# Two equal tiles handled in one operation in the recurrent branch, and the norms' reciprocal root as a square root and a reciprocal

## The reference

```python
h = rmsnorm(x, norm_mix)                 # x * rsqrt(mean(x^2) + 1e-6) * g
u_pool | u_rnn | u_gate | g_pool | g_rnn = h @ w_in
y_pool = pool_mixer(u_pool) @ w_pool_out
v  = conv4(u_rnn)                        # causal, per channel, 4 taps
r, i = sigmoid(v @ w_a + b_a), sigmoid(v @ w_x + b_x)     # 8 heads of 128 x 128
a  = exp(-8 r softplus(-lam));  b = sqrt(1 - a^2) * i * v
hr_t = a_t * hr_(t-1) + b_t              # along the sequence
y_rnn = (hr * gelu(u_gate)) @ w_rnn_out
x  = x + (sigmoid(g_pool) * y_pool + sigmoid(g_rnn) * y_rnn) @ w_o
h  = rmsnorm(x, norm_ffn);  x = x + (silu(h @ w_gate) * (h @ w_up)) @ w_down    # 2816 wide
out = rmsnorm(x, norm_final)
```

## Time and profile before

| | us |
|---|---|
| median of 3 runs (lowest, highest) | 1024.84 (1024.12, 1025.46) |
| profiled execution, device time | 1024.35 |
| its span, slowest core (core 3, role b) | 1022.8 |
| PE / DVE / ACT / POOL busy on core 3 | 924.4 / 591.4 / 556.7 / 336.8 |

### The profile page before, as it was taken

One profiled execution on the slowest core, in us unless ns is written; L12 is line 12 of the kernel. 1 busy time (PEld: TensorE's weight loads), 2 busy tenths in 40 slices (PEclk: granted clock), 3 DMA queues, 4 the chain that ended last, 5 costly groups with the idle time before them and its releaser, 6 DMA issues.

```text
span 1022.8 us, 13708 instructions; the slowest of 8 cores (1016.8 to 1022.8 us)
## 1 busy us (share of the span) xinstructions
PE 924.4 (90%) x4484; PEld 446.6 (44%) x4484; DVE 591.4 (58%) x798; ACT 556.7 (54%) x804; POOL 336.8 (33%) x347
## 2 busy tenths in 40 slices
PE   2378688698978999999999999999999999999995
PEld 1134233233433444444444444444555555555553
DVE  2179998999999867844253544533644452222235
ACT  2579997989889942548264938611722351111112
POOL 2438593778655641151001122112251211000000
PEclk8579789899989999999999999999999999999998
DMA  8921452003644276768403257255939175910003
GB/s 176 242 69 33 160 93 42 12 1 55 116 82 87 38 192 118 160 98 150 82 8 56 39 80 141 44 101 123 253 69 212 30 129 108 211 41 2 1 1 135
DMA packets 42765, 96.88 MB, mean 95 GB/s; under 512 B 3776, under 2 KB 19264, under 8 KB 42560
## 3 DMA queue, kind: packets, MB, share of 16 engines
q0 software_dynamic: 23904, 63.45, 36.1%
q1 hardware_dynamic: 18784, 32.48, 10.6%
HBM read 151.75 MB, written 7.60 MB: 156 GB/s over the span
## 4 chain that ended last, share of the span: by engine, by line
PE 78%; ACT 9%; issue 5%; POOL 3%; DVE 2%; DMA 2%; ACTq 0%; DVEq 0%; SPq 0%; POOLq 0%
PE bank L705 74%; PE bank L770 2%; PE bank L667 2%; DMA wu<-w_in 2%; ACT th L780 1%; DVE v L757 1%; ACT q L798 1%; POOL sq L638 1%; ACT th L788 1%; ACT v L745 1%; ACT L798 1%; ACT L780 1%; DMA xt<-xT 1%; POOL vb L765 1%; ACT wi L780 0%
## 5 line engine op out<-in xcount | busy, mean ns | idle before, releaser
L705 PE MATMUL bank<-h,wf 128*128 128x508 bf16 (+2 forms) x1408 | 280.7, 358 | 0.0
L705 PEld LDWEIGHTS bank<-h,wf 128*128 128x128 bf16 x1408 | 136.5, 97 | 139.9 <-issue 0.8
L757 DVE SCALAR_TENSOR_TENSOR v<-bank,keep_cst,v 128x496 f32<-128x496 f32 (+3 forms) x200 | 128.8, 683 | 32.4 <-POOL v L754 13.4
L705 PE MATMUL bank<-h,wu 128*128 128x500 bf16 (+4 forms) x576 | 130.1, 381 | 16.3 <-DMA wu<-w_in 11.0
L1084 DVE TENSOR_TENSOR ff<-tf,bank 128x508 bf16<-128x508 f32 (+2 forms) x88 | 55.7, 634 | 147.9 <-PE bank L705 123.5
L705 PE MATMUL bank<-ff,wz 128*128 128x508 bf16 (+2 forms) x704 | 139.5, 359 | 0.0
L1079 ACT ACTIVATE tf<-bank 128x508 f32<-128x508 f32 (+2 forms) x88 | 48.8, 557 | 137.8 <-PE bank L705 134.4
L652 ACT ACTIVATE sq<-x 128x508 f32<-128x508 f32 (+2 forms) x56 | 32.9, 590 | 125.3 <-DVE x L1096 97.4
L705 PEld LDWEIGHTS bank<-ff,wz 128*128 128x128 bf16 x704 | 68.9, 98 | 68.6 <-issue 0.5
L705 PEld LDWEIGHTS bank<-h,wu 128*128 128x128 bf16 x576 | 58.7, 103 | 83.9 <-issue 32.9
L765 POOL CAST vb<-v 128x496 bf16<-128x496 f32 (+3 forms) x68 | 61.1, 905 | 61.4 <-DVE v L757 53.3
(11 more groups left out here) (103 smaller groups left out, 1311.7 us busy)
## 6 DMA issues: line engine op xcount, KB each, us to landing
wf<-wfi POOLq DMA_DIRECT2D x44, 512.0 KB, 9.5
wz<-wfo POOLq DMA_DIRECT2D x16, 704.0 KB, 10.1
xt<-xT SPq DMA_DIRECT2D x16, 500.0 KB, 8.6
wu<-w_in POOLq DMA_DIRECT2D x16, 256.0 KB, 13.7
xt<-xT SPq DMA_DIRECT2D x8, 512.0 KB, 21.1
wa<-w_in POOLq DMA_DIRECT2D x16, 256.0 KB, 5.9
wg<-w_in POOLq DMA_DIRECT2D x16, 256.0 KB, 5.4
wb<-w_in POOLq DMA_DIRECT2D x16, 256.0 KB, 5.5
```

Source lines behind the costliest of these rows:

```text
L705: last = e.matmul(p.tensor[:, 0:n], lhsT=wap(kc), rhs=rhs(kc), start=(kc == 0), stop=(kc == K - 1))
L757: g.op("dve", c_dve(w), k, lambda e, p=p, o=o, w=w, s=s: e.scalar_tensor_tensor(out=v.tensor[:, o:o + w], in0=p.tensor[:, HALO - s:HALO - ...
```

## The change

1. `rnn_pair` (new): where a group has exactly two tiles of one width, and neither the extra tap on POOL (`tap`) nor the PSUM variant (`ps`) is on, both tiles' u groups are written to two neighbouring banks, and each operation on ACT, DVE and POOL up to the tanh is issued once for both. The matmuls stay one per tile.
2. The norm's root: ACT's Sqrt in place in PSUM, then DVE's reciprocal in place, for Ln and Exp on ACT. All norms are changed, 18 in role a and 17 in role b.
3. The gate weights `rg` are loaded in four pieces of two heads, the first in the head, the others when their heads are due. PSUM is one tensor of eight banks; single banks are taken beside occupied ones so that pairs stay free.
4. New tables of numbers. Role b: prefix groups of one, two and two tiles (256; 496 + 496; 496 + 496), own tiles 508 + 508 and 420 + 420, the extra tap for two heads of the last chunk (before: all eight), the PSUM variant off. Role a: tiles 256, 352, 396 and 344, 500, 392 (before 256, 412, 396 and 344, 500, 332); never two tiles in a group, so nothing is joined there.

```diff
+    def find_bank(self, b, t):
+        free = [self.bank_live[i] is None and self.banks[i][0] <= t for i in range(8)]
+        if b.space == "ps2":
+            c = [(max(self.banks[i][0], self.banks[i + 1][0]), i) for i in range(0, 8, 2) if free[i] and free[i + 1]]
+        else:
+            c = [(self.bank_live[i ^ 1] is None, self.banks[i][0], i) for i in range(8) if free[i]]
+        return min(c)[-1] if c else None
...
-                head.append(self.load("pool", rg, lambda: rg.tensor[:], dr["rg"], 128 * 2048 * 4, K, "rg"))
+                head.append(self.load_rg(0, K))
+    def load_rg(self, i, key):
+        b = self.rg[i]
+        return self.load("pool", b, lambda: b.tensor[:], self.dr["rg"][:, 2 * i:2 * i + 2], 128 * 512 * 4, key, "rg")
...
-        ln = self.buf("ln", [w])
-        g.op("act", c_act(w, 1), key, lambda e: e.activation(out=ln.tensor[:], in_=pss.tensor[:, 0:w], func=AF.Ln,
-                                                             bias=self.eps.tensor[:, 0:1]), rd=[pss, self.eps], wr=[ln],
-             table=LN, tag=tag + "ln")
-        g.op("act", c_act(w), key, lambda e: e.activation(out=pss.tensor[:, 0:w], in_=ln.tensor[:], func=AF.Exp, scale=-0.5),
-             rd=[ln], wr=[pss], table=EXPL, tag=tag + "rs")
+        g.op("act", c_act(w, 1), key, lambda e: e.activation(out=pss.tensor[:, 0:w], in_=pss.tensor[:, 0:w], func=AF.Sqrt,
+                                                             bias=self.eps.tensor[:, 0:1]), rd=[pss, self.eps], wr=[pss],
+             table=SQRT, tag=tag + "rs")
+        g.op("dve", c_dve(w), key, lambda e: e.reciprocal(out=pss.tensor[:, 0:w], in_=pss.tensor[:, 0:w]), rd=[pss], wr=[pss], tag=tag + "rc")
...
+        both = len(tiles) == 2 and tiles[0][1] == tiles[1][1] and not (ps or on[2] or on[5])
+        if both:
+            self.rnn_pair(j, tiles, wu, key, toff, v, th, wi, kk_vb)
...
+    def rnn_pair(self, j, tiles, wu, key, toff, v, th, wi, cast):
+        two = lambda b: b.tensor[:].rearrange("p (t w) -> p t w", t=2)
+        p = self.banks("ps_u")
...
+        for s in (1, 2, 3):
+            g.op("dve", c_dve(2 * w), k, lambda e, s=s: e.scalar_tensor_tensor(
+                out=two(v), in0=p.tensor[:, :, HALO - s:HALO - s + w],
+                scalar=cst.tensor[:, C_CW + 8 * (3 - s) + j:C_CW + 8 * (3 - s) + j + 1], in1=two(v),
+                op0=ALU.mult, op1=ALU.add), rd=pk + [cst] + vk, wr=vk, tag="cv")
...
+        for q, hcol, dst in ((0, 0, th), (1, 8, wi)):
+            pg = self.banks("ps_g")
+            for i in range(2):
+                g.op("pe", c_mm(w) + 0.05, k + 1 + 0.3 * q, lambda e, pg=pg, q=q, i=i: e.matmul(
+                    pg.tensor[:, i, 0:w], lhsT=self.rg[j // 2].tensor[:, j % 2, q, :], rhs=vb.tensor[:, i * w:i * w + w], start=True, stop=True),
+                    rd=[vb, self.rg[j // 2]], wr=[(pg, i)], tag="gt")
+            g.op("act", c_act(2 * w, 1), k + 1 + 0.3 * q, lambda e, pg=pg, dst=dst, hcol=hcol: e.activation(
+                out=two(dst), in_=pg.tensor[:, :, 0:w], func=AF.Tanh, scale=0.5,
+                bias=self.hb.tensor[:, hcol + j:hcol + j + 1]), rd=[(pg, 0), (pg, 1), self.hb], wr=[(dst, 0), (dst, 1)], table=TANH, tag="th")
...
-        prefix=[256, 496, 496, 496, 496], groups=[2, 2, 1], own=[[508, 508], [460, 380]], wp=261.84, window2=107.54,
+        prefix=[256, 496, 496, 496, 496], groups=[1, 2, 2], own=[[508, 508], [420, 420]], wp=294.7, window2=309.7,
```

More of the change, by code:

```diff
@@ L164, in can_alloc @@
                 continue
-            if b.space == "ps":
-                if not any(self.bank_live[i] is None and self.banks[i][0] <= t for i in range(8)):
+            if b.space != "sb":
+                if self.find_bank(b, t) is None:
                     return False
@@ L169, in can_alloc @@
                 n += b.nbytes
-        if room and any(b.space == "ps" and b.left is not None for b in o.bufs):
+        if room and any(b.space != "sb" and b.left is not None for b in o.bufs):
             room = 0
@@ L179, in do_alloc @@
             b.left = b.uses
-            if b.space == "ps":
-                c = [(self.banks[i][0], i) for i in range(8) if self.bank_live[i] is None and self.banks[i][0] <= t]
-                _, i = min(c)
-                self.bank_live[i] = b
-                b.off = i
-                extra += self.banks[i][1]
+            if b.space != "sb":
+                i = b.off = self.find_bank(b, t)
+                for x in range(i, i + (2 if b.space == "ps2" else 1)):
+                    self.bank_live[x] = b
+                    extra += self.banks[x][1]
             else:
@@ L203, in finish_refs @@
                         us[u.eng] = u
-                    self.banks[b.off] = (b.dead + self.prm["bank_lag"], list(us.values()))
+                    for x in range(b.off, b.off + (2 if b.space == "ps2" else 1)):
+                        self.bank_live[x] = None
+                        self.banks[x] = (b.dead + self.prm["bank_lag"], list(us.values()))
                 elif b.name.startswith("keep"):
@@ L542, in start @@
         self.xt0 = self.tile8("xt", W0 + HALO)
-        self.rg = rg = self.buf("keep_rg", [2, 8, 128], BF16)
+        self.rg = [self.buf("keep_rg", [2, 2, 128], BF16) for _ in range(4)]
         head = self.load_tile(self.xt0, 0, W0 + HALO, -99, "xt")
@@ L700, in norm1_tile, with mm_group @@
         return h
[L702 removed]
+    def mm_group(self, p, n, wb, rhs, rd, key, tag, K=8, wap=None, half=None):
         def f(e):
             for kc in range(K):
[L705 removed]
+                last = e.matmul(p.tensor[:, 0:n] if half is None else p.tensor[:, half, 0:n], lhsT=wap(kc), rhs=rhs(kc), start=(kc == 0), stop=(kc == K - 1))
             return last
[L707 removed]
+        return self.g.op("pe", K * c_mm(n), key, f, rd=rd + [wb], wr=[p if half is None else (p, half)], tag=tag)
     def proj(self, wb, h, w, key, tag, halo=False, sl=None):
@@ L737, in rnn_group @@
         off = 0
-        for i, (h, w, part) in enumerate(tiles):
+        both = len(tiles) == 2 and tiles[0][1] == tiles[1][1] and not (ps or on[2] or on[5])
+        if both:
+            self.rnn_pair(j, tiles, wu, key, toff, v, th, wi, kk_vb)
+        for i, (h, w, part) in enumerate([] if both else tiles):
             k = key + toff * i
@@ L941, in build @@
         P = prm.get("pre")
+        base, step = (P["rnn"][0] if P else prm["keys"][0]["rnn"])[:2]
+        for i in range(1, 4):
+            self.load_rg(i, base + step * 2 * i - prm["lead"])
         for i, w in enumerate(prm["prefix"]):
@@ L1197, in build_program @@
     with ExitStack() as es:
-        ps = [es.enter_context(nc.psum_tensor("bank%d" % i, [128, 512], F32)) for i in range(8)]
+        ps = es.enter_context(nc.psum_tensor("bank", [128, 8, 512], F32))
         sems = {e: es.enter_context(nc.semaphore("s_" + e)) for e in ENGINES}
@@ L1213, in build_program @@
                     seen.add(id(b))
-                    if b.space == "ps":
-                        b.tensor = ps[b.off]
+                    if b.space != "sb":
+                        b.tensor = ps[:, b.off, :] if b.space == "ps" else ps[:, b.off:b.off + 2, :]
                     else:
```

95 lines of the change are left out of this document (55 added, 40 removed).

## The result

| | us |
|---|---|
| before, median of 4 runs beside it (lowest, highest) | 1024.52 (1024.12, 1025.46) |
| after, median of 4 runs (lowest, highest) | 1067.22 (1064.49, 1068.62) |
| after / before | 1.0408, 95% interval 1.0388 to 1.0429 |
| profiled execution of after | 1066.01, span 1064.2 (core 5, role b) |

What follows compares the result with a forecast made beforehand. DVE, with ACT close behind, was taken to pace role b before about 350 us. -12.5 - 6 + 21.7 - 2 + 4.1 + 4.2 = 9.5 us on 1024.35 gave 1034; range 1015 to 1046, own case 1028 to 1044.

Steps and rivals of the forecast that it cites:

- the gain of 20.5 us: Role b's three gains together: 12.5 us from joined taps, 6 from ACT, 2 from the start.
- At one pass: Rival: reciprocals cost one or two passes; role b's sum becomes -16 us, role a ends last, about 1018; chance 0.24.
- what I called covered: Role b: first two of the stage's seven reciprocals hidden by other waits; later norms hidden behind 68 matmuls or more.
- Joined taps, -12.5: Role b's DVE-paced stage: 72 fewer DVE instructions at 0.17 us each give 12.5 us less.
- the pair as a delay: Rival: late fifth weight and waiting for two norms cost 8 us at role b's start; 1044, up to 1050; chance 0.13.
- ACT, -6: Role b's stage: ACT stops being a second bound; 6 us less, between 0 and 8, bounded by DVE's waits for ACT.
- Start, -2: Role b's start: later first wide tap against DVE work done earlier; 2 us less, from 8 less to 8 more.
- eight passes: Assumed DVE reciprocal cost, 4.3 us at 500 columns; five in role b's stage add 21.7 us; own case, chance 0.50.
- the sign: The whole kernel gets slower, given chance 0.67; faster 0.25, within 0.2% 0.08.
- the hole ahead of the first `wf` group: Role b after the stage: PE stands 4.1 us since only 32 `wo` matmuls cover the second norm's chain.
- The tail's sum: Role b behind the last matmul: wider last tile, reciprocal for Exp and less cover; together 4.2 us more.
- the first `wr` at 367 to 372 us: Expected sign in role b: when PE starts its first `wr` matmul at the stage's end; 367.7 before the change.

Runs made afterwards that it cites:

- e1: Kernel after, same instruction order, each reciprocal replaced by a one-pass multiplication by 1.0 (values differ): 1033.1 us, 1.0084 of before.
- e9: Kernel after with Ln and Exp for the norms, joined pairs kept, role a's old tile widths, order searched anew: 1.0125 of before.
- e13: Kernel after with nothing joined, Ln and Exp for the norms, role a's old tile widths, order searched anew: 1.0026 of before.
- e2: Kernel after, same order, but DVE takes its role's branch ahead of the first reciprocal: 1.0401 of before.
- e3: Kernel after, same order, but rg loaded in one transfer in the head, not four pieces: 1.0340 of before.
- e12: Kernel after, same order, with one pass for each reciprocal and rg in one transfer: 1.0072 of before.
- e11: Kernel after with its reciprocals, role a's old tile widths, order searched anew with the reciprocal's measured price: 1.0190 of before.
- e6: Kernel after, same order, with Ln and Exp on ACT again in place of root and reciprocal: 1.0173 of before.

## Why the prediction was wrong

**The step that failed is the gain of 20.5 us that I set against the reciprocals: 12.5 for the joined taps, 6 for ACT, 2 for the start.** At one pass I had role b 16 us faster; e1 measures that case as 8.6 us slower, an error of 25 of the 33 us that the forecast missed. The other 8 lie in what I called covered among the reciprocals.

- *Joined taps, -12.5.* The count and the rows were right (72 fewer instructions, 1.24 us each), and in place the pairs are worth 9 to 10 us. The price was taken as path, though, since DVE was busy for 95% of the stretch. A pair also has to wait for both of its halves, and the order for pairs in the groups [1, 2, 2] holds that wait: DVE's 10.5 us came back as idle time (e9 against e13), 6.8 of them at the first taps, and the kernel lost 10. I had this rival ("the pair as a delay") with 0.13 and put it at the start alone.
- *ACT, -6.* ACT's work fell as forecast (84 table loads on core 5 for my 86, 38 us less busy in the stretch), and no run shows a gain from it: DVE's wait for ACT's first product, which bounded the gain, rose from 4.6 to 11.3 us on core 5 of after, e9 alike:

```profile
DVE v L874 <- ACT v L869: 11.3, 5, 6.8
```

- *Start, -2.* The first wide tap came at 98.0, not at some 81 (64.5, 8 more, and two reciprocals of 4.3). DVE had done 30 us more by then (46.5 us busy up to 98.0, before 16.6 up to 64.5), 8.3 of them in three reciprocals; so 11.8 us are lost there, 3.5 of them as idle time. The branch is not in it (e2); rg is, with up to 7 us on the slowest core, as long as the reciprocals fill DVE (e3, e12).

**The reciprocals.** Per instruction I was too high (4.3 for 3.27 us at 500), in total too low: from eight passes to one I reckoned 25.4 us, and from six measured passes to one it was 33 to 34 (e1). The error is in what I called covered. The first two were to hide in DVE's idle start, but its idle time up to the first wide tap did not shrink (47.9 us before, 51.5 now). Between the first `wr` and the last `wz` I had one hole of 4.1 us and the later norms hidden behind 68 matmuls or more; instead 11.0 of the 34 us came off that stretch, and PE waited at three of the later `h` and two `x` norms, 0.3 to 0.9 us each. In role a I allowed 2 to 4 us for that, and PE's idle time between 50 and 1000 us went from 2.2 to 14.3 us on core 0:

```profile
50.00:1000.00 950.00, 935.70 (x5798) 565.18 (x5797) 519.79 (x753) 413.52 (x692) 202.91 (x244) 1.00 0.42 84
```

A reason stood in the diff, and I did not use it: the planner was told 0.68 us for an instruction that takes 3.27, so the cover that I counted on was planned for less. Telling it, with a new search, took 22 us back (e11).

**Right were** the sign, the hole ahead of the first `wf` group (4.1 forecast, 3.5 measured), the taps' rows and the number of reciprocals. The tail's sum (4.2 forecast, 4.3 measured) is in part luck: Exp's place took 2.3 us more by the reciprocal, not 3.05, and what made up for it is no term of mine, the norm's two matmuls at a granted clock of 0.50 (1.74 us for 0.88). Wrong was the first `wr` at 367 to 372 us. PE also stood idle for 12.8 us ahead of it, where before `wb` matmuls filled the time; its first ten products then took 0.44 us each, where eleven took 2.52 in all, 0.23 each. That is the lower level of 1.2 GHz for 2.4 (granted clock 0.50 from 388.06 to 392.25 and 0.99 from there to 400):

```profile
388.06 4.39 PE L719 MATMUL bank<-gl,wr 128*128 128x508 bf16 x10 [12.77 <-DVE gl L855]
```

In differences of the table, the 41.8 us are 24.1 for the swap in this order (after against e6), 4.9 for the order (e6 against e9), 10.1 for the pairs in these groups (e9 against e13) and 2.7 for the rest (e13). The first is a held comparison. The other steps compare orders that were searched, and a few us of an order's luck may be in them; how e6's 17.7 divide among groups, widths and table for the kernel's own order stays open.

## What to carry to other kernels

An instruction that replaces two on another engine is priced by its own row, and where an order is planned, the planner must get that price: with 3.3 us in place of a wrong 0.7, and a new search, 22 us came back here. Joining two operations saves their fixed part, but can lose it again where something waits for the first half; undo it in place, and also give the single form an order of its own, before calling it a gain. Busy time that falls on the engine that sets the pace is a gain only if its idle time doesn't rise by as much.
